# A four-layer inference step on one core: the state-space layer's decay tiles made ahead, its masks as selects, its weight halves split by two engines

## What is computed

```python
def ssd_scan(x, dt, a, bm, cm, h0):
    tri = jnp.tril(jnp.ones((q, q), bool))
    def step(hs, inp):
        xc, dtc, bc, cc = inp
        acs = jnp.cumsum(dtc * a, axis=1)
        seg = acs[:, :, None, :] - acs[:, None, :, :]
        lmat = jnp.exp(jnp.where(tri, seg, -jnp.inf))
        cb = jnp.einsum('bign,bjgn->bijg', cc, bc)
        mm = cb[..., None] * lmat * dtc
        y = jnp.einsum('bijgr,bjgrp->bigrp', mm, xg)
        y = y + jnp.einsum('bign,bgrpn->bigrp', cc, hg) * jnp.exp(acs)
        w_end = jnp.exp(acs[:, -1:, :] - acs) * dtc
        h_new = hs * jnp.exp(acs[:, -1]) + jnp.einsum('bjgn,bjgr,bjgrp->bgrpn', bc, w_end, xg)
        return h_new, y

def ssd_mixer(h, w_in, ...):
    z, xbc, dt = jnp.split(h @ w_in, ...)
    xbc = silu(centred_dwconv(xbc, conv_w, conv_b))        # x, B, C: four taps
    dt = softplus(dt + dt_bias); a = -jnp.exp(a_log)
    y_f, h_f = ssd_scan(xs, dt[:, :, 0], a[0], bm, cm, h0[:, 0])
    y_b, h_b = ssd_scan(flip(xs), flip(dt[:, :, 1]), a[1], flip(bm), flip(cm), h0[:, 1])
    y = y_f + flip(y_b) + d_skip[:, None] * xs
    return rmsnorm(y * silu(z), norm_g) @ w_out, ...
```

## Time and profile before

| | us |
|---|---|
| median of three runs | 3276.47 |
| lowest, highest | 3271.76, 3278.17 |
| profiled execution | 3272.87 |
| its span | 3271.4 |
| SSD groups, from the state transposes of group 0 to the sum of squares (723.78 to 1375.74) | 651.96 |
| PE busy over the span | 2761.7 |
| POOL busy over the span | 1366.2 |
| DVE busy over the span | 1258.7 |
| ACT busy over the span | 900.8 |

### The profile page before, as it was taken

One profiled execution on the slowest core, in us unless ns is written; L12 is line 12 of the kernel. 1 busy time (PEld: TensorE's weight loads), 2 busy tenths in 40 slices (PEclk: granted clock), 3 DMA queues, 4 the chain that ended last, 5 costly groups with the idle time before them and its releaser, 6 DMA issues.

```text
span 3271.4 us, 40340 instructions
## 1 busy us (share of the span) xinstructions
PE 2761.7 (84%) x16233; PEld 2242.1 (69%) x16233; DVE 1258.7 (38%) x1874; ACT 900.8 (28%) x1717; POOL 1366.2 (42%) x831
## 2 busy tenths in 40 slices
PE   6769998978787788598699899899898688699887
PEld 4666665877777778497695694784874678655557
DVE  1424444365555555433312412423323113344452
ACT  1213333143333444411221221231311101233321
POOL 0523333645555554442351641641632544234442
PEclk6889999888888899698699999999999898899998
DMA  7112221324343442131120221121221232100011
GB/s 247 43 49 56 68 68 37 113 74 129 118 119 115 129 121 86 48 100 56 37 67 34 78 86 39 66 73 41 76 73 52 71 100 52 34 19 20 21 45 58
DMA packets 293161, 238.79 MB, mean 73 GB/s; under 512 B 60879, under 2 KB 276497, under 8 KB 291461
## 3 DMA queue, kind: packets, MB, share of 16 engines
q1 hardware_dynamic: 285584, 200.38, 20.7%
q10 hardware_dynamic: 2404, 21.22, 1.6%
q0 software_dynamic: 5008, 14.81, 1.3%
HBM read 212.28 MB, written 24.09 MB: 72 GB/s over the span
## 4 chain that ended last, share of the span: by engine, by line
PE 67%; DVE 14%; ACT 6%; POOL 6%; issue 4%; DMA 1%; POOLq 1%; ACTq 0%; DVEq 0%; SPq 0%
PE ps L245 12%; PE ps L246 11%; PE ps L247 11%; PE ps L990 5%; PE ps L2052 3%; PE ps L960 3%; PE ps L2063 2%; PE ps L1996 2%; POOL w_hi L267 2%; PE ps L1264 2%; DVE room L1569 2%; PE ps L1267 2%; PE ps L2012 2%; PE ps L1268 2%; PE ps L982 2%
## 5 line engine op out<-in xcount | busy, mean ns | idle before, releaser
L267 POOL TENSOR_TENSOR w_hi<-ring,ones 128x1024 fp32r<-128x1024 f32 (+1 forms) x190 | 385.0, 2027 | 587.4 <-DMA ring<-in_ssd_w_in_dram 170.8
L268 POOL TENSOR_TENSOR w_lo<-ring,w_hi 128x1024 fp32r<-128x1024 f32 (+1 forms) x190 | 478.5, 2518 | 14.9
L245 PE MATMUL ps<-room_r,w_hi 128*128 128x320 f32 (+1 forms) x1280 | 413.4, 323 | 79.5 <-DVE room_r L630 36.9
L246 PE MATMUL ps<-room_r,w_hi 128*128 128x320 f32 (+1 forms) x1280 | 405.6, 317 | 0.0
L247 PE MATMUL ps<-room_r,w_lo 128*128 128x320 f32 (+1 forms) x1280 | 405.1, 316 | 0.0
L245 PE MATMUL ps<-h_hi,w_hi 128*128 128x320 f32 x992 | 322.5, 325 | 74.4 <-DVE h_lo L545 44.8
L246 PE MATMUL ps<-h_lo,w_hi 128*128 128x320 f32 x992 | 316.6, 319 | 0.0
L247 PE MATMUL ps<-h_hi,w_lo 128*128 128x320 f32 x992 | 316.0, 319 | 0.0
L1079 POOL TENSOR_TENSOR room<-room 128x640 f32<-128x640 f32 (+1 forms) x160 | 167.9, 1083 | 354.1 <-DVE room L1045 353.7
L245 PEld LDWEIGHTS ps<-room_r,w_hi 128*128 128x128 f32 x1280 | 248.1, 194 | 86.8 <-issue 63.6
L1264 PE MATMUL ps<-h_hi,w_hi 128*128 128x320 f32 x736 | 253.4, 344 | 2.0 <-POOL w_lo L268 2.0
(11 more groups left out here) (329 smaller groups left out, 4990.0 us busy)
## 6 DMA issues: line engine op xcount, KB each, us to landing
ring<-in_ada_w_dram SPq DMA_DIRECT2D x24, 1024.0 KB, 5.2
ring<-in_ssd_w_in_dram SPq DMA_DIRECT2D x48, 512.0 KB, 4.8
yT<-in_ada_w_dram SPq DMA_DIRECT2D x24, 1024.0 KB, 8.0
...
```

The costliest lines, as they stand in the source:

```text
L245: pe.matmul(dst, a_hi, b_hi, start=start, stop=False)
L246: pe.matmul(dst, a_hi, b_lo, start=False, stop=False)
L267: pool_t.after(pool.tensor_tensor(hi, raw, one.broadcast_to(raw.shape), ALU.mult))
L268: pool.tensor_tensor(lo, raw, hi.bitcast(F32), ALU.subtract).then_inc(w_split, 1)
```

## The change

The decays get buffers of their own. `s_e` (two buffers) now takes the broadcast rows, is masked and exponentiated in place, and the sum of its two directions goes to `s_m` (three buffers, half as wide). `s_ce` (three buffers) is loaded a second time from the same rows, for chunks 1 to 4 only. The room comes from `s_raw` and `s_xe`, which go from three buffers to two, and from `s_acc`, which is halved. The loop that made everything of chunk pos in one place is taken apart: `decay` and the new `grow` on ACT, and `both`, `weights` and `outer` on DVE. Decays 0 to 3 of group g+1 are written inside group g; group 0 makes its own at its start.

The mask becomes two selects on POOL. The high half of three slabs per group is now made by ACT (`split_high`), the low one stays on POOL (`split_low`). On PE, one half of a projection tile goes ahead of the updates, so that each item after it stands one half later, and the sums of the ada units stand behind a chunk.

```diff
-        s_raw, s_xc = b_(3, RAW), b_(8, CONV)
+        s_raw, s_xc = b_(2, RAW), b_(8, CONV)
-        s_xe = b_(3, 2, GX)
+        s_xe = b_(2, 2, GX)
-        s_acc = b_(2, TOK)
-        s_m, s_ce = b_(2, 8, P), b_(3, 8, P)
+        s_acc = b_(TOK)
+        s_e, m_at = b_(2, 8, P), b_.at
+        s_m, wd_at = b_(3, GH, P), b_.at
+        s_ce = b_(3, 8, P)
@@ ssd_sync
+            def load_e(g, pos):
+                q = NT * g + pos
+                if g < GROUPS:
+                    if q >= 2:
+                        sp.wait_ge(S["s_added"], q - 1)
+                    load_rows(s_e[:, q % 2], g, CHUNKS[pos], S[f"s_e_loaded{q % 2}"])
+            def load_c(g, pos):
+                i = LC * g + pos - 1
+                if g < GROUPS:
+                    if i >= 3:
+                        sp.wait_ge(S["s_y_done"], NT * ((i - 3) // LC) + (i - 3) % LC + 2)
+                    load_rows(s_ce[:, i % 3], g, CHUNKS[pos], S[f"s_c_loaded{i % 3}"])
-            load_rows(0, 0)
-            load_rows(0, 1)
+            load_e(0, 0)
+            load_e(0, 1)
+            for pos in (1, 2, 3):
+                load_c(0, pos)
             for g in range(GROUPS):
                 load_slab("z", g)
+                if g == 0:
+                    load_e(0, 2)
+                    load_e(0, 3)
+                load_e(g, 4)
                 load_unit(g, 0)
@@ ssd_act
+        def split_high(act, kind, g):
+            slot, full, _ = place[kind, g]
+            for h in range(2):
+                act.wait_ge(w_loaded[slot][h], full[h])
+                act.activation(w_hi[:, slot, h * HALF:(h + 1) * HALF], ring[:, slot, h * HALF:(h + 1) * HALF], ACT.Copy
+                               ).then_inc(S["s_high"], 1)
+            def grow(g, pos):
+                i = LC * g + pos - 1
+                if g < GROUPS:
+                    act.wait_ge(S[f"s_c_loaded{i % 3}"], 32 * (i // 3) + 32)
+                    act.activation(s_ce[:, i % 3], s_ce[:, i % 3], ACT.Exp).then_inc(S["s_ce_exp"], 1)
                 silu("x0", g)
+                split_high(act, "z", g)
                 silu("x1", g)
@@ ssd_act, group 0, ahead of first_tap B
+                    for pos in range(4):
+                        decay(g, pos)
+                    grow(g, 1)
+                    grow(g, 2)
@@ ssd_dve
+            def both(g, pos):
+                q = NT * g + pos
+                dve.wait_ge(S["s_decayed"], q + 1)
+                if q >= 3:
+                    dve.wait_ge(S["s_y_done"], q - 2)
+                e = s_e[:, q % 2]
+                dve.tensor_tensor(s_m[:, q % 3], e[:, 0:GH], e[:, GH:], ALU.add).then_inc(S["s_added"], 1)
+            def outer(g, pos):
+                i, tt = LC * g + pos - 1, CHUNKS[pos]
+                dve.wait_ge(S["s_ce_exp"], i + 1)
@@ ssd_pool
+            def split_low(kind, g):
+                for h in range(2):
+                    pool.wait_ge(S["s_high"], HIGHS[kind, g] + h + 1)
+                    pool.tensor_tensor(lo, raw, hi.bitcast(F32), ALU.subtract).then_inc(w_split, 1)
             def mask(g, pos):
-                pool.wait_ge(S[f"s_rows_loaded{q % 3}"], 32 * (q // 3) + 32)
-                if q >= 2:
-                    pool.wait_ge(S["s_y_done"], q - 1)
-                pool.tensor_tensor(m, r, neg[:].unsqueeze(2).broadcast_to([P, 2, GH, P]), ALU.add
-                                   ).then_inc(S["s_masked"], 1)
+                pool.wait_ge(S[f"s_e_loaded{q % 2}"], 32 * (q // 2) + 32)
+                for d in range(2):
+                    e = s_e[:, q % 2, d * GH:(d + 1) * GH]
+                    ins = pool.affine_select(out=e, in_=e, compare_op=ALU.is_ge, fill=-BIG, base=0,
+                                             pattern=[[0, GH], [1 - 2 * d, P]], channel_multiplier=2 * d - 1)
+                ins.then_inc(S["s_masked"], 1)
```

198 lines of the change are left out of this document (112 added, 86 removed).

## The result

| | before | after |
|---|---|---|
| median us | 3277.23 (4 runs) | 3372.60 (4 runs, 3368.29 to 3377.47) |
| ratio | | 1.0295, 95% interval 1.0277 to 1.0313 |
| profiled execution, its span | 3272.87, 3271.4 | 3368.29, 3366.4 |

The changed kernel is 95 us slower, where the forecast said 34.5 us, and it lies outside the range of 3258 to 3350. The direction and the chain of three waits were as forecast; the size was not, and in one stretch of a group the forecast also had the wrong engine as the bound. The page of after, part 1, against the earlier trace rows: DVE and POOL work less, ACT more, and PE is busy for 14 us longer, though the SSD groups have the same matmuls.

A forecast was written before the change was run, and what follows sets the result against it. The prediction took groups to be bound by a chain of chunk read, mask, decay, DVE, next chunk. Its terms 5 + 19 + 20 - 9.5 gave +34.5 us, so 3311 us, range 3258 to 3350.

The forecast's parts named there:

- steps 2 to 4: In each group PE idles 8.9 us before chunk 3, 6.4 before chunk 4 and 3.0 at the next group's first turn.
- step 5: From the first turn to the end of the next chunk 1 only PE binds; the group ends at 87.8 us.
- step 1: The last load of rows, queued on SP behind an ada unit, load_c and slab BC, lands 13.5 us after chunk 1.
- steps 3 and 4: Freed buffer, load (5.2 us), mask, decay, then first tap: chunk 4 starts at 35.1 us, the next turn at 54.7.
- group 0: Layer start: ten row loads before slab z cost +8 us, decays before B's first tap +11; together +19.
- six groups, from chunk 1 to chunk 1: A group lasts 87.8 us against 87.0 before, as old waits go and new ones come: +5 us.
- group 6: It keeps the waits, shortened, and PE idles 12.8 us before z0 of group 7: +20 us.
- group 7: Decays 0 to 3 are ready, so it takes 46 us, not 55.5: -9.5 us with the halved sum of squares.
- 2: chunk 3 starts: Mask, decay, grow and outer product precede chunk 2's reading on DVE, so chunk 3 starts at 20.1 us.
- The loads of rows in steps 3 and 4: Rival: these loads take 8.1 us, not 5.2; group 93.6 us, total 3346; chance 0.13 shared with dear selects.
- The dear selects: Rival: POOL's mask selects cost 1.17 us each; group 90.8 us, total 3329; chance 0.13 shared with late loads.
- the bound moves to PE: Rival: without the waits before chunks 3 and 4, group 70.5 us, total 3194; chance 0.15 including one wait gone.

The follow-up runs named there:

- rows_early: Changed kernel with SP issuing load_e(g+1, 1) ahead of load_c(g, 4) and slab BC: 3346.0 us, ratio 1.0206 to before.
- all_in: Changed kernel with DVE, ACT and SP reordered, ada units spread on PE, group 0 reordered, group 7's z earlier, x's high half later: 3189.3 us.
- chain_cut: Changed kernel with outer(g, 4) and x0's taps behind the readings of chunks 2 and 3 on DVE, grow(g, 4) before decay(g+1, 1) on ACT: 3290.5 us.

## Why the prediction was wrong

The three waits of steps 2 to 4 were found in the trace, in their places and with the releasers that the forecast names. Two things failed: the sentence of step 5 that "nothing binds but PE", and the sizes of step 1, steps 3 and 4, and group 0. The sum fell short by 61 us.

| term | forecast | measured |
|---|---|---|
| start of the state transposes of group 0 | 0 | -3.3 |
| group 0, from there to its chunk 1 | +19 | +31.1 |
| six groups, from chunk 1 to chunk 1 | +5 | +54.5 |
| group 6 | +20 | +19.9 |
| group 7 | -9.5 | -7.6 |

Group 6: 58.04 us from its chunk 1 to the next state transposes, forecast 58.2, with PE's wait before z0 at 12.5, forecast 12.8. Group 7: 47.9 us instead of 55.5, forecast 46.

**The groups.** In us behind the end of chunk 1, for group 2 (981.0):

| step | forecast | measured |
|---|---|---|
| 1: last load, mask 1 starts | 13.5 | 15.3 |
| 2: chunk 3 starts | 20.1 | 22.0 |
| 3: mask 2 starts | 26.0 | 27.6 |
| 3: chunk 4 starts | 35.1 | 38.3 |
| 4: first turn | 54.7 | 58.9 |
| 5: from there to the next chunk 1's end | 33.1 | 36.8 |
| period | 87.8 | 95.7 |

- Step 1 was sized 1.8 too low. SP took 3.40 us to issue slab BC and 4.08 for the two loads of rows behind it, where the forecast took 0.5 for an issue, so that the loads were out at 10.2 and not at 5. Its own bound from the bytes was 14.4, and it took 13.5. rows_early shows what the place in the queue is worth, 5.7 us. By the Trainium skill's fit in DMA: Bandwidth & Descriptors, section Anatomy of one DMA, the load would, as an estimate, have come at 10.3; the page measured that fit for single transfers issued by GpSimd, these are several behind each other on SP's queue, and the trace has 15.3.
- Steps 3 and 4 were sized 1.3 and 1.0 too low. I took 2.75 for taps and 0.7 for a sum, but they now meet POOL's low half of slab BC: 4.70 and 2.33 us. I had the 4.70 in the earlier trace rows and priced it at 0.6 in all.
- Step 5 was wrong in its sentence: "nothing binds but PE". DVE does, held by POOL's low half of x. x_late, which moves ACT's high half of x and so that low half, and nothing else, takes the stretch from 36.6 us on average to 31.7, and all_in from 37.3 to 31.5. The Trainium skill, SBUF — State Buffer, section SBUF: two separate sides, says that the pair of ports is an exclusive lock for a whole instruction; the rows of L1662 and L1807 agree (5.17 beside 4.93 us). I had cited the rule for what POOL's lighter load gives, and not asked where the halves that stay on POOL would fall. The rows of before had a warning too: the 3.14 us before the update, and the 2.48 before the final state, are among the 16.4 us of waits that the forecast lets go, and no step says why they should.

These sum to 7.8 us of group 2's period; over all six groups 8.3 us of a period were missing. The same shortfall by kind, per group on average: PE's waits are 23.9 us and not 18.3 (10.3 before chunk 3, 6.5 before chunk 4, 3.9 at the turn, against 8.9, 6.4 and 3.0, and 3.2 before update 2 and the final state, against nothing), and its matmuls take 72.2 us. The forecast leaves 69.5 for them, less than the 70.6 of before, though it adds waits.

**The base.** Of a group's +9.1 only 0.8 was forecast because two large terms cancel: waits of 16.4 that go, waits of 18.3 that come. An error of 10% in steps that make 88 us is 9 us a group. The range of 78 to 97 for a group held the 96.1, but the range for the sum was cut at 3350.

**Group 0.** The forecast gave +8 before the turn and +11 before `half(4)`; the waits there were 12.7 and 10.6. For the first, ten loads of rows took 10.3 us to issue and not 5. The sum also left out a piece of work: chunk 1 now has one half of a tile more ahead of it, 3.6 us. The forecast has this half's absence in its 58.2 for group 6 and not its presence in group 0. The rest of the 31.1 are slower matmuls, some 5 us (granted clock 0.74 in this stretch, 0.90 before), less 1 us of other waits.

**Rivals.** The loads of rows in steps 3 and 4 did not come late. In group 2, from the end of the sum that frees the buffer to the select it was 5.2 us (1003.42 to 1008.62) and 5.1 (1021.44 to 1026.58), as forecast, and not 8.1. So that the period is near this rival's 93.6 says nothing for it.

```profile
1002.73 0.69 DVE L1687 TENSOR_TENSOR room<-room 128x512 f32<-128x512 f32 x1
1019.11 2.33 DVE L1687 TENSOR_TENSOR room<-room 128x512 f32<-128x512 f32 x1
```

```profile
1008.62 1.23 POOL L1817 TENSOR_SCALAR_AFFINE_SELECT room<-room 128x512 f32<-128x512 f32 x2 [11.08 <-DMA room<-acs_rows]
1026.58 1.23 POOL L1817 TENSOR_SCALAR_AFFINE_SELECT room<-room 128x512 f32<-128x512 f32 x2 [5.69 <-DMA room<-acs_rows]
```

The dear selects did not come: two selects of 512 columns took 1.22 us, forecast 1.3. That the bound moves to PE needs more than two waits: with both gone (chain_cut) a group takes 86.4, not 70.5, because ada transfers and copies stood right behind. Of that the forecast had no term at all.

The halved sum of squares (2.50 us on PE instead of 4.63) gave nothing: from its start to the output projection it is 21.3 us in both kernels, since PE waits for DVE there.
